# Delta rule's gate rows: spread over the partitions by transfers between places on the chip, in place of picks by TensorE

## The reference, cut to what matters

```python
beta = pad_front(jax.nn.sigmoid(b_a))
g = pad_front(-jnp.exp(a_log) * jax.nn.softplus(a_a + dt_bias))
G = jnp.cumsum(g, axis=-1)                     # within a chunk
diff = G[..., :, None] - G[..., None, :]
gamma = jnp.where(incl, jnp.exp(jnp.where(incl, diff, 0.0)), 0.0)
k_beta = k * beta[..., None]
a_mat = jnp.where(strict, jnp.einsum('bnhcd,bnhsd->bnhcs', k_beta, k) * gamma, 0.0) + jnp.eye(CHUNK)
rhs = jnp.concatenate([v * beta[..., None], k_beta * jnp.exp(G)[..., None]], axis=-1)
sol = lax.linalg.triangular_solve(a_mat, rhs, left_side=True, lower=True, unit_diagonal=True)
q_dec = q * jnp.exp(G)[..., None]
chunk_dec = jnp.exp(G[..., -1])
```

## Time and profile before

| | us |
|---|---|
| median of 3 runs | 1841.1 (1838.98 to 1842.49) |
| the profiled execution | 1846.39 |
| its span | 1845.1 |
| convolution, first to last step | about 713 to 794 |
| delta rule, first group | about 806 to 930 |
| delta rule, second group | about 930 to 1030 |

### The profile page before, as it was taken

The page is one execution under the profiler, slowest core; times in us unless marked ns, Lnnn a source line. Parts: engine busy times, 40 slices in busy tenths (PEclk is TensorE's granted clock), DMA queues, the critical chain, the costliest instruction groups (busy, mean ns, idle before and its releaser), DMA issues.

```text
span 1845.1 us, 23154 instructions
## 1 busy us (share of the span) xinstructions
PE 1705.1 (92%) x9262; PEld 1296.8 (70%) x9262; DVE 1187.9 (64%) x2131; ACT 752.1 (41%) x1324; POOL 400.0 (22%) x343
## 2 busy tenths in 40 slices
PE   8999999999999999999999999988788788878888
PEld 7979988977799888989999989863333333333333
DVE  5676654765566547864262666689777766777855
ACT  4655533444355436774363655442222121122211
POOL 0220000000000000002012000335545544544551
PEclk9999999999999999999899999998989878988899
DMA  6336555444455553532231224799999999999997
GB/s 252 135 117 213 189 184 183 176 167 160 160 182 184 183 183 137 183 118 79 82 115 47 107 100 173 283 382 418 422 421 421 422 421 421 422 421 421 421 422 311
DMA packets 62955, 453.85 MB, mean 246 GB/s; under 512 B 7000, under 2 KB 7128, under 8 KB 8448
## 3 DMA queue, kind: packets, MB, share of 16 engines
q0 software_dynamic: 37152, 268.45, 35.1%
q1 hardware_dynamic: 25040, 178.27, 27.0%
q10 hardware_dynamic: 656, 5.66, 0.9%
HBM read 451.15 MB, written 1.05 MB: 245 GB/s over the span
## 4 chain that ended last, share of the span: by engine, by line
PE 68%; DMA 14%; DVE 8%; ACT 4%; POOL 3%; issue 2%; another core or an unknown queue 0%; DVEq 0%; ACTq 0%; POOLq 0%
PE banks L625 16%; PE banks L627 16%; PE banks L626 16%; DMA uv_rows<-expert_uv,index 14%; PE banks L2539 10%; DVE uv_rows L2725 3%; POOL uv_rows L2755 3%; ACT weights_hi L602 1%; PE banks L1970 1%; PE banks L1959 1%; DVE weights_lo L611 1%; PE banks L1690 1%; PE banks L1952 1%; ACT diag L2604 1%; PE banks L2313 0%
## 5 line engine op out<-in xcount | busy, mean ns | idle before, releaser
L2539 PE MATMUL banks<-uv_rows,diag 128*128 128x512 f32 x1024 | 509.0, 660 | 110.2 <-ACT diag L2604 110.2
L611 DVE TENSOR_TENSOR weights_lo<-weights,weights_hi 128x1024 fp32r<-128x1024 f32 x325 | 397.1, 1263 | 252.0 <-ACT weights_hi L602 252.0
L2539 PEld LDWEIGHTS banks<-uv_rows,diag 128*128 128x128 f32 x1024 | 214.6, 213 | 403.2 <-issue 273.1
L602 ACT ACTIVATE weights_hi<-weights 128x1024 fp32r<-128x1024 f32 x328 | 328.9, 1052 | 357.4 <-PE banks L627 340.9
L625 PE MATMUL banks<-x_hi,weights_hi 128*128 128x256 f32 (+1 forms) x1472 | 426.6, 290 | 5.0 <-DVE weights_lo L611 1.4
L627 PE MATMUL banks<-x_hi,weights_lo 128*128 128x256 f32 (+1 forms) x1472 | 419.7, 285 | 0.0
L626 PE MATMUL banks<-x_lo,weights_hi 128*128 128x256 f32 (+1 forms) x1472 | 419.3, 285 | 0.0
L2725 DVE CUSTOM_DVE_ANT_0 uv_rows<-uv_rows,tokens 128x1024 f32<-128x1024 f32 x256 | 305.5, 1223 | 147.1 <-DMA uv_rows<-expert_uv,index 147.0
L2755 POOL DMA_INDIRECT uv_rows<-expert_uv,index x254 | 315.5, 1242 | 309.2 <-PE banks L2539 256.1
L625 PEld LDWEIGHTS banks<-x_hi,weights_hi 128*128 128x128 f32 x1472 | 281.1, 191 | 12.1 <-DVE weights_lo L611 3.1
L627 PEld LDWEIGHTS banks<-x_hi,weights_lo 128*128 128x128 f32 x1472 | 280.9, 191 | 0.0
(11 more groups left out here) (384 smaller groups left out, 2073.4 us busy)
## 6 DMA issues: line engine op xcount, KB each, us to landing
weights<-weights SPq DMA_DIRECT2D x164, 1024.0 KB, 4.8
uv_rows<-weights SPq DMA_DIRECT2D x4, 1024.0 KB, 7.7
uv_rows<-expert_uv,index POOLq DMA_INDIRECT x254, 17.5
sb_first<-constants_first ACTq DMA_DIRECT2D x1, 1920.0 KB, 9.5
sb_always<-constants_always ACTq DMA_DIRECT2D x1, 1627.5 KB, 7.2
sb_peer<-constants_peer ACTq DMA_DIRECT2D x1, 1544.0 KB, 8.0
h<-x SPq DMA_DIRECT2D x1, 1024.0 KB, 5.8
out<-h SPq DMA_DIRECT2D x4, 256.0 KB, 4.6
```

Of the source, the lines that this page charges most:

```text
L602: self.act.activation(self.w_hi[b % SLOTS][:, f], raw[:, f], ACT.Copy).then_inc(self.hi_made, 1)
L611: self.dve.tensor_tensor(self.w_lo[b % SLOTS][:, f], self.landing(b)[0][:, f], self.w_hi[b % SLOTS][:, f], ALU.subtract).then_inc(self.lo_ ...
L2539: mm = pe.matmul(self.bank(2 * t + half), self.diag[:, k, :], self.uv[ROW_BUFFER[n]][:, f], start=(u < NT and k == 0), stop=(u >= UNITS - ...
```

## The change

The 24 picks of the delta rule go, with their semaphore. Each head's rows of beta and G, now neighbours in `lam`, are written to all 128 partitions of a new tile `d_rows` by one transfer, and its row of exp(G) to a part of `lam` that is free by then by another; both read one partition of `lam` 128 times. SP issues these eight transfers for the first group ahead of block 9 of the convolution, and eight for the second group ahead of block 8 of `fa_qkv`, in the queue of the weights. ScalarE copies only `ncum`, once. VectorE reads the rows from SBUF in place of the banks. `d_rows` shares its place with `gates_a`, hence a wait of ScalarE. The order of the rows in `LAM` changes, and with it the numbers given to `token_scalar`.

```diff
@@ SP @@
+CONV_AT = sum(n for _, n in STREAM[:10])
+SPREAD_AT = (CONV_AT + 9, CONV_AT + 12 + 8)
...
                 self.sp.wait_ge(self.lo_made, PARTS * (b - SLOTS + 1))
+            if b in SPREAD_AT:
+                self.sync_spread(SPREAD_AT.index(b))
             self.sp.dma_start(self.raw[b % SLOTS][:, :], w[b]).then_inc(self.block_full[b % SLOTS], 16)
...
-    LAM = ("beta", "G", "nbe", "tail", "eG", "ncum", "y", "t", "u", "g")
+    LAM = ("nbe", "tail", "beta", "G", "eG", "ncum", "y", "t", "u", "g")
+    SPREAD = 16 * 2 * HG
+
+    def sync_spread(self, group):
+        sp, beta, eg, kept = self.sp, self.LAM.index("beta"), self.LAM.index("eG"), self.LAM.index("ncum") + 1
+        if group == 0:
+            sp.wait_ge(self.lam_ready, 1)
+            sp.wait_ge(self.lam_eg, 1)
+            sp.wait_ge(self.h_normed, NT)
+        else:
+            sp.wait_ge(self.d["rows_used"].sem, self.d["rows_used"].at(0, 3))
+        for hh in range(HG):
+            h = group * HG + hh
+            sp.dma_start(self.d_rows[:, hh], self.lam[h:h + 1, None, beta:beta + 2, :].to_broadcast([1, P, 2, SM])).then_inc(self.rows_spread, 16)
+            sp.dma_start(self.lam[:, kept + hh, :], self.lam[h:h + 1, None, eg, :].to_broadcast([1, P, SM])).then_inc(self.rows_spread, 16)
+
+    def rows_landed(self, group):
+        return self.rows_spread, 16 + (group + 1) * self.SPREAD

     def scalar_spread(self):
+        at = self.LAM.index("ncum")
         self.act.wait_ge(self.lam_ready, 1)
-        for j in range(1, 4):
-            self.act.dma_start(self.lam[j * QUARTER:j * QUARTER + H2, 0:6, :], self.lam[0:H2, 0:6, :]).then_inc(self.rows_spread, 16)
+        self.act.dma_start(self.lam[QUARTER:QUARTER + H2, at, :], self.lam[0:H2, at, :]).then_inc(self.rows_spread, 16)
@@ scalar_fill @@
+        if name == "gates" and c == 0:
+            act.wait_ge(self.d["rows_used"].sem, self.d["rows_used"].at(1, 3))
@@ tensor_delta @@
-        if group == 0:
-            pe.wait_ge(self.rows_spread, 16 * 3)
-        for j, name in enumerate(("G", "beta", "eG")):
-            if j:
-                wait("rows_used", j)
-            for hh in range(HG):
-                h = group * HG + hh
-                mm = self.tensor_pick(self.bank(hh, SM), name, h, hh, SM)
-            mm.then_inc(d["rows"].sem, 1)
+        for j in range(3):
             fill(j)
-        wait("rows_used", 3)
+        wait("rows_used", 2)
@@ vector_delta @@
-        rows = self.banks(0, HG, SM)
-        wait("rows", 1)
+        beta, rows = self.d_rows[:, :, 0, :], self.lam[:, self.LAM.index("ncum") + 1:, :]
+        dve.wait_ge(*self.rows_landed(group))
...
-                g = dve.tensor_scalar(self.d_gam[0:n, hh, c:c + n], self.bank(hh)[0:n, c:c + n],
-                                      self.token_scalar(t, 1, group * HG + hh), 0.0, ALU.subtract, ALU.min)
+                g = dve.tensor_scalar(self.d_gam[0:n, hh, c:c + n], self.d_rows[0:n, hh, 1, c:c + n],
+                                      self.token_scalar(t, 3, group * HG + hh), 0.0, ALU.subtract, ALU.min)
...
-        wait("rows", 2)
-        dve.tensor_tensor(self.d_kb[:, :, :], k, rows, ALU.mult).then_inc(d["rows_used"].sem, 1)
+        if group == 0:
+            dve.wait_ge(self.rms_scaled.sem, self.rms_scaled.at("conv", 8))
+        dve.tensor_tensor(self.d_kb[:, :, :], k, beta, ALU.mult).then_inc(d["rows_used"].sem, 1)
         fill(1)
-        wait("rows", 3)
@@ tensor_forgetting @@
                 if i == 0:
+                    pe.wait_ge(*self.rows_landed(1))
```

More of the change, by code:

```diff
@@ L382, in memory @@
         self.fa_qkv = self.place("fa_qkv", [P, 3 * H2, SM])
+        at = self.top
+        self.d_rows = self.place("drows", [P, HG, 2, SM])
+        self.top = at
         self.y[0], self.y[1] = self.place("gates_a", [P, KD, S]), self.y[0]
@@ L525, in signals @@
         self.rows_spread = nc.alloc_semaphore("rows_spread")
-        names = {"rows": 3, "rows_used": 3, "gam": 3, "prod": 3, "prod_used": 3, "turn": 3, "turn_used": 3, "masked": 3, "attn": 2,
+        names = {"rows_used": 3, "gam": 3, "prod": 3, "prod_used": 3, "turn": 3, "turn_used": 3, "masked": 3, "attn": 2,
                  "back": 3, "A": 3, "T0": 3, "B": 13, "M": 15, "M1": 15, "Z": 15, "T": 15, "ks": 2,
@@ L2029, in scalar_delta @@
                 h, f = group * HG + hh, slice(hh * P, (hh + 1) * P)
-                act.activation(self.d_ktail[0:n, t, f], self.bank(2)[0:n, f], ACT.Copy, scale=self.token_scalar(t, 3, h))
-                made = act.activation(self.d_bv[0:n, t, f], self.bank(3)[0:n, f], ACT.Copy, scale=self.token_scalar(t, 0, h))
+                act.activation(self.d_ktail[0:n, t, f], self.bank(2)[0:n, f], ACT.Copy, scale=self.token_scalar(t, 1, h))
+                made = act.activation(self.d_bv[0:n, t, f], self.bank(3)[0:n, f], ACT.Copy, scale=self.token_scalar(t, 2, h))
             made.then_inc(d["turn_used"].sem, 1)
@@ L2139, in vector_delta @@
                 for hh in range(HG):
-                    x = dve.scalar_tensor_tensor(self.d_rhs[:, H[hh]], ks[:, H[hh]], self.token_scalar(t, 2, group * HG + hh),
+                    x = dve.scalar_tensor_tensor(self.d_rhs[:, H[hh]], ks[:, H[hh]], self.token_scalar(t, 0, group * HG + hh),
                                                  self.d_bv[:, t, H[hh]], ALU.mult, ALU.add)
```

## The result

The changed kernel takes 1948.9 us, median of four runs (1948.7 to 1949.95), against 1841.8 us (1839.0 to 1842.9) for the kernel before in the same session: ratio 1.0574, 95% interval 1.0561 to 1.0587. The forecast was 1939, with 1905 to 1960 as the likeliest case's own range and 1838 to 1960 as the whole. The profiled execution took 1948.7 us.

A forecast was written before the change was run, and what follows sets the result against it. TensorE, 92% busy, bounds the kernel, and whatever starves it costs full length; stalls 53.1 + 42.8, restarts 3.0, less gain 1.3, add 97.6 us to 1841.1, giving 1938.7 us (1939), range 1838 to 1960.

The forecast's parts named there:

- likeliest case: Added transfers limited by reading four neighbouring partitions through one port, stalling the weights behind them: 1938.7 us, chance 0.62.
- X: Time one group's added transfers hold SP's queue: 58.0 us at 28.8 GB/s, bounds 43.5 and 62.8.
- the hidden case: Rival: only the writing side is limited, transfers take about 4 us inside the slack; 1839.8 us, chance 0.26.
- the case of packets at a fixed price: Rival: each small packet costs about 0.2 us, 13 us for a group's transfers; 1849.4 us, chance 0.12.
- The slack: Time in hand for the weight block behind the transfers: 4.9 us at the first place, 15.2 at the second.
- Counting nothing more behind the second split: At the second place no slack beyond ScalarE's split, since TensorE waits on moves queued behind it: 15.2 us stays.
- SP's extra issues run beside the transfer: SP's eight added issues per group, 0.33 us each, overlap the transfer.
- The restarts: TensorE at a lowered clock after each of two stalls: 1.5 us each, 3.0 together, bounds 0 and 6.
- The gain: Time saved by removing the picks: 0.5 + 0.1 + 0.7 = 1.3 us, bounds 0 and 5.8.
- The subtractions' 0.5: VectorE's twelve gate subtractions after the first group's second set, reading SBUF instead of PSUM: 0.5 us saved, bounds 0 and 1.35.
- the second group's first set: Picks that TensorE runs straight into after the outputs' last matmul, with bank free and block made: worth 0.7 us.
- the sets counted at nothing: Picks of the first group's first and second sets and the second group's other two, under other waits: worth 0.

The follow-up runs named there:

- first experiment: Changed kernel with the sixteen transfers reading gate rows that ScalarE first stored outside the core, still in SP's queue: 1842.7 us, ratio 0.9994 to the kernel before.
- in two stages: Changed kernel with each row copied first to partitions 0 to 31, then from these to the other three quarters: 1870.4 us, ratio 1.0136 to the kernel before.
- The version that gets it without a stall: Changed kernel with rows read from outside the core and transfers issued through GpSimd's queue: 1840.6 us, ratio 0.9990 to the kernel before.

## Why the prediction was right

**The bound and the mechanism**: right in the main. The time is set by 1.67 MB per group that are read from four neighbouring partitions ahead of the weights. Taking away the narrow source alone removes it (first experiment), a wider one inside SBUF shortens X to 22 us (in two stages), so the hidden case and the case of packets at a fixed price both fall. That the queue is shared matters less than the prediction had it: by GpSimd's queue 83 of the 107 us remain, since the DMA engines themselves are held. That the reading side is the narrow one was a choice which the rows didn't decide, as the prediction says; with the writing side the same working gave 1840. To this extent the figure came out by luck, and the whole range, 1838 to 1960, is wide because of it. The rate was read from a transfer of the kernel before: 28.8 GB/s, against 27.1 measured.

**X**: 58.0 us forecast, 60.8 and 61.0 measured (landings 823.2 and 967.65, against 762.36 and 850.68 + 55.96). This is the term that was mis-sized, by 5% and twice over. The row gave 38.4 and 28.8 GB/s in its two windows and I took the lower; both were above the steady rate. The row was a weak one: its windows overlap by 0.1 us and hold nine large packets each where a transfer has eight, and that four packets run at a time was assumed. With the 27.2 GB/s of the Trainium skill (SBUF — State Buffer, section "Door 1: The DMA port swizzle (why `[64,N]` ≈ `[32,N]`)") the prediction had 61.4 us, nearer to the measured 60.8 and 61.0.

**The slack**: right. Wait of ScalarE = X less what lay between landing and split before: 60.8 - 2.4 = 58.4 (58.70 measured), TensorE's 60.8 - 4.9 = 55.9 (56.04), and at the second place 61.0 - 15.2 = 45.8 (45.76). Counting nothing more behind the second split was right, for TensorE's 45.25 follow it directly.

**SP's extra issues run beside the transfer**: wrong. SP's 0.33 us for an issue was read from rows in which no slow transfer stood ahead. The first two took 0.56 and 0.60 us and the others 5 to 10 us. Here it cost nothing beyond X, since SP had only those weights to issue. In a kernel where SP has other work behind such transfers, it would.

**The restarts**: 1.5 us each forecast, 58.11 - 56.04 = 2.1 and 48.92 - 45.76 = 3.2 measured, the second with the small products of the solve at the lower clock level, 1.2 GHz (granted clock 0.50 from 968 to 976). Together that is 5.2 where 3.0 were forecast, 2.2 us too little.

**The gain**: 1.3 us forecast, 2.07 + 0.13 + 0.84 = 3.0 measured. The subtractions' 0.5 is 0.57, and the second group's first set is worth 0.84 where I had 0.7; the sets counted at nothing gave nothing beyond that. What was left out is the clock behind the second set (1.5 us): the prediction priced a fallen clock for the stalls and didn't ask whether the change would also remove one. The clock stayed up in this place in all nine traces without the picks; against them stands one trace with the picks. Why it stayed up, when the idle time in front of it was 1.51 us and not 1.41, isn't shown.

**The sum.** Forecast 53.1 + 42.8 + 3.0 - 1.3 = 97.6. Measured by the same terms 56.0 + 45.8 + 5.2 - 3.0 = 104.0; less the 3.0 us of clock that differed between the two profiled executions and with 1.3 from later stages that is the 102.3 between the spans. The medians lie 107.1 apart, because the profiled execution before was 4.6 us above its median and the one after on it. So of the 9.5 us between the forecast 97.6 and the 107.1, 6.4 are the terms above; the other 3.1 are differences between executions, which no trace here assigns.

**Whether there is a kernel to be had.** The picks' removal alone is worth some 3 us, 0.16%, by the table, half of it the clock behind the second set. The version that gets it without a stall has the ratio 0.9990 with an interval that holds both 1 and that value: a gain is likely by the trace, not shown by the clock. Most of the picks stood in gaps.

## What to carry to other kernels

A transfer that copies one partition's row to all 128 is priced by its source: bytes written divided by about 27 GB/s, and most of that time can be taken from the other queues too, since the DMA engines are held by it. Ahead of a stream that another engine waits for, it was paid in full here, less the slack at that place; so read the slack at each candidate place, divide the transfers among several, or take the rows from outside the core, where the same 1.67 MB cost some 5 us. And before an operation is moved off the tensor engine, look at what its own wait is for: of six sets of picks only one stood on the path for more than 0.13 us, and the larger part of the gain came from a wait and a clock beside them.

## What the runs showed of the hardware that was not expected

- The issue of a transfer can hold its engine for the transfer's length: 5.15 and 10.29 us on SP, against 0.43 for most of the same transfers from outside the core. GpSimd issued the slow ones in 0.55 to 0.81 us each (from 747.5 to 752.1).
- Transfers at 27 GB/s keep 87 to 95% of 16 DMA engines' time, and a weight block in another queue then lands 10 to 60 us after its issue, against 5 to 6.
- Two queues with slow transfers did not take turns packet by packet: for some 20 us only one of them moved anything, then the other.
- The granted clock differs between executions in a stretch with the same work: between moves 18 and 24 of the table the changed kernel took 3.0 us less than the kernel before, the two-stage kernel 1.4 less, and the one with rows from outside the core through GpSimd's queue 4.5 less, though none of them differs there in what is computed.
